# A decoder trunk on one core: the values' product moves both weight parts at once, and ScalarE scales its corrections

## What is computed

```python
qkv = h @ w_qkv
q, k, v = jnp.split(qkv, 3, axis=-1)
...
s_own = s_own - slopes[None, None, :, None] * dist_own.astype(jnp.float32)[None, :, None, :]
s_own = jnp.where((dist_own >= 0)[None, :, None, :], s_own, NEG)
...
p = jax.nn.softmax(scores, axis=-1)
...
return o @ w_o
```

## Time and profile before

| | us |
|---|---|
| median of 3 runs | 876.34 (876.16 to 876.99) |
| the profiled execution | 877.2 |
| its span, first to last instruction | 875.2 |
| PE busy | 866.4 (99%) |
| PEld busy | 756.4 (86%) |
| DVE busy | 648.8 (74%) |
| ACT busy | 467.5 (53%) |
| HBM read | 157.84 MB, 182 GB/s over the span |

### The profile page before, as it was taken

One profiled execution on the slowest core, in us unless ns is written; L12 is line 12 of the kernel. 1 busy time (PEld: TensorE's weight loads), 2 busy tenths in 40 slices (PEclk: granted clock), 3 DMA queues, 4 the chain that ended last, 5 costly groups with the idle time before them and its releaser, 6 DMA issues.

```text
span 875.2 us, 12263 instructions
## 1 busy us (share of the span) xinstructions
PE 866.4 (99%) x5103; PEld 756.4 (86%) x5103; DVE 648.8 (74%) x760; ACT 467.5 (53%) x550; POOL 22.7 (3%) x49
## 2 busy tenths in 40 slices
PE   9999999999999999999999999999999999999997
PEld 7888888888889988888888888888888988888886
DVE  6898776567987699777655697777656998777452
ACT  6765555435656665555534375555544665555441
POOL 1000005200000000000000000000000000000000
PEclk9999999999999999999999999999999999999999
DMA  7777555563644447665556566665555377565431
GB/s 238 245 243 239 192 180 169 186 206 98 220 145 145 145 143 242 193 192 181 174 187 193 180 191 197 191 191 184 172 194 172 98 240 234 185 214 184 147 118 48
DMA packets 154534, 159.67 MB, mean 182 GB/s; under 512 B 3000, under 2 KB 152816, under 8 KB 154480
## 3 DMA queue, kind: packets, MB, share of 16 engines
q1 hardware_dynamic: 154128, 158.35, 56.6%
q10 hardware_dynamic: 352, 0.55, 0.2%
HBM read 157.84 MB, written 1.05 MB: 182 GB/s over the span
## 4 chain that ended last, share of the span: by engine, by line
PE 91%; DVE 5%; DMA 1%; ACT 1%; issue 1%; SPq 0%; ACTq 0%; DVEq 0%
PE psum L455 90%; DVE w_lo L1098 2%; DMA raw<-in_ffn_w_gate_dram 1%; ACT w_hi L863 1%; DMA band<-in_x_dram 1%; PE psum L782 1%; DVE score L1393 0%; PE psum L765 0%; DVE neg_max L1398 0%; DVE neg_max L1397 0%; SPq L390 0%; PE psum L485 0%; PE psum L645 0%; DVE soft L1406 0%; DVE scratch L1374 0%
## 5 line engine op out<-in xcount | busy, mean ns | idle before, releaser
L455 PE MATMUL psum<-xg,w_hi 128*128 128x512 f32 x1536 | 484.5, 397 | 0.3 <-DVE w_lo L1098 0.3
L1098 DVE TENSOR_TENSOR w_lo<-raw,w_hi 128x2048 fp32r<-128x2048 f32 (+1 forms) x148 | 330.1, 2231 | 106.0 <-ACT w_hi L863 106.0
L455 PEld LDWEIGHTS psum<-xg,w_lo 128*128 128x128 f32 x1536 | 288.6, 188 | 68.2
L863 ACT ACTIVATE w_hi<-raw 128x2048 fp32r<-128x2048 f32 x149 | 278.0, 1867 | 116.9 <-PE psum L455 112.0
L455 PE MATMUL psum<-xg,w_lo 128*128 128x256 f32 x1536 | 301.9, 278 | 0.0
L455 PEld LDWEIGHTS psum<-xg,w_hi 128*128 128x128 f32 x1536 | 234.0, 189 | 2.7 <-issue 1.3
L455 PE MATMUL psum<-h_all,w_hi 128*128 128x512 f32 (+1 forms) x656 | 189.4, 374 | 0.0
L455 PEld LDWEIGHTS psum<-h_all,w_lo 128*128 128x128 f32 x592 | 111.4, 188 | 23.4
L455 PE MATMUL psum<-h_all,w_lo 128*128 128x256 f32 x592 | 121.8, 278 | 0.0
L455 PEld LDWEIGHTS psum<-h_all,w_hi 128*128 128x128 f32 x656 | 100.2, 189 | 0.8 <-issue 0.8
L900 ACT ACTIVATE scratch<-psum 128x512 f32<-128x512 f32 x44 | 26.1, 593 | 79.5 <-PE psum L455 79.5
(11 more groups left out here) (116 smaller groups left out, 494.0 us busy)
## 6 DMA issues: line engine op xcount, KB each, us to landing
raw<-in_ffn_w_gate_dram SPq DMA_DIRECT2D x42, 1024.0 KB, 5.3
raw<-in_ffn_w_up_dram SPq DMA_DIRECT2D x42, 1024.0 KB, 5.3
raw<-in_ffn_w_down_dram SPq DMA_DIRECT2D x24, 1024.0 KB, 5.1
raw<-in_attn_w_qkv_dram SPq DMA_DIRECT2D x12, 1024.0 KB, 5.1
raw<-in_ffn_w_down_dram SPq DMA_DIRECT2D x20, 512.0 KB, 4.2
raw<-in_ffn_w_down_dram SPq DMA_DIRECT2D x12, 768.0 KB, 4.4
raw<-in_attn_w_o_dram SPq DMA_DIRECT2D x4, 1024.0 KB, 5.7
raw<-in_ffn_w_gate_dram SPq DMA_DIRECT2D x7, 256.0 KB, 6.0
```

The source lines that it names most:

```text
L455: return nc.tensor.matmul(out, stationary, moving, start=start, stop=stop, skip_group_check=True)
L863: nc.scalar.activation(w_hi[:, n % SPL, 0:size], raw[:, n % RAW, 0:size], ACT.Copy).then_inc(hi_split, 1)
L1098: nc.vector.tensor_tensor(w_lo[:, n % SPL, 0:size], raw[:, n % RAW, 0:size], w_hi[:, n % SPL, 0:size].bitcast(f32), ALU.subtract).then_inc ...
```

## The change

`w_hi` and `w_lo` become the two halves of one tensor `w_parts`, so that a slice can take the same chunk of both. The values' product moves both parts of a chunk through the high activations in one matmul of 512 columns, and the high weights through the low activations in one of 256, which adds to the second half of the accumulator. Two chunks are taken together: two matmuls of 512, then two of 256. The accumulator is now a whole bank for each t: banks 6 and 7 (quad 0), 0 and 1 (quads 1 and 2), 4 and 5 (quad 3). ScalarE scales the second half (the corrections) into `v_sb`, `scale_v_corrections`, and VectorE scales the first half and adds the two. Waits go with the banks: V3 waits for the copies of the probabilities in banks 4 and 5 and no longer for the query scaling, and the wait for V3's scaling moves from the second scores of pass 3 to the front of `out_tile(0)`.

```diff
-        w_hi = sb("w_hi", [P, SPL, ROWS], f32r)
-        w_lo = sb("w_lo", [P, SPL, ROWS], f32r)
+        w_parts = sb("w_parts", [P, 2, SPL, ROWS], f32r)
+        w_hi, w_lo = w_parts[:, 0], w_parts[:, 1]
...
-            return psum[:, 0, t * GW:(t + 1) * GW] if j else psum[:, 6 + t, 0:GW]
+            first_bank = 6 if j == 0 else 4 if j == QUADS - 1 else 0
+            return psum[:, first_bank + t, :]
...
-                elif j:
+                elif 0 < j < QUADS - 1:
                     pe.wait_ge(qkv_scaled, 3 * j + 1)
...
-                hi, lo = col_tile(w_hi, n), col_tile(w_lo, n)
+                hi = col_tile(w_hi, n)
+                both = w_parts[:, :, n % SPL, :].rearrange("p s (k f) -> p s k f", k=DC)
                 for t in range(TT):
                     toks = slice(t * P, (t + 1) * P)
-                    for k in range(DC):
-                        out = v_acc(j, t)
-                        mm(out, xg_hi[:, k, toks], hi[:, k, :], start=(k == 0))
-                        mm(out, xg_hi[:, k, toks], lo[:, k, :])
-                        last = mm(out, xg_lo[:, k, toks], hi[:, k, :], stop=(k == DC - 1))
+                    if j == QUADS - 1:
+                        pe.wait_ge(probT_copied, QH * (j - 1) + t + 1)
+                    for k0 in range(0, DC, 2):
+                        for k in (k0, k0 + 1):
+                            mm(v_acc(j, t).rearrange("p (s f) -> p s f", s=2), xg_hi[:, k, toks], both[:, :, k, :],
+                               start=(k == 0))
+                        for k in (k0, k0 + 1):
+                            last = mm(v_acc(j, t)[:, GW:2 * GW], xg_lo[:, k, toks], hi[:, k, :], stop=(k == DC - 1))
...
             def out_tile(j, halfway=None):
                 n = ATT0 + 3 * QUADS + j
                 weights(n)
+                if j == 0:
+                    pe.wait_ge(qkv_scaled, 3 * QUADS)
...
                     pe.wait_ge(o_lo_done, j)
-                    pe.wait_ge(qkv_scaled, 3 * QUADS)
...
+            def scale_v_corrections(j):
+                act.wait_ge(consts_built, CONSTS)
+                act.wait_ge(rstd_done, 2)
+                for t in range(TT):
+                    if j == 0 and t == 0:
+                        act.wait_ge(first_v, 1)
+                    else:
+                        act.wait_ge(tile_used, ATT0 + 3 * j + 3)
+                    nc.scalar.activation(v_sb[:, j % 2, t, :], v_acc(j, t)[:, GW:2 * GW], ACT.Copy,
+                                         scale=rstd_p[:, t:t + 1]).then_inc(v_corr, 1)
...
             split_hi(ATT0 + SPL)
+            scale_v_corrections(0)
             split_hi(ATT0 + 1 + SPL)
...
+                if j < QUADS - 1:
+                    scale_v_corrections(j + 1)
                 split_hi(ATT0 + 3 * j + 4 + SPL)
                 act.wait_ge(pv_done, QH * (j + 1))
...
-                        if j == 0 and t == 0:
-                            dve.wait_ge(first_v, 1)
-                        else:
-                            dve.wait_ge(tile_used, ATT0 + 3 * j + s + 1)
-                        ins = nc.vector.tensor_scalar(v_sb[:, j % 2, t, :], v_acc(j, t),
-                                                      rstd_p[:, t:t + 1], None, ALU.mult)
+                        dve.wait_ge(v_corr, TT * j + t + 1)
+                        ins = nc.vector.scalar_tensor_tensor(out=v_sb[:, j % 2, t, :], in0=v_acc(j, t)[:, 0:GW],
+                                                             scalar=rstd_p[:, t:t + 1], in1=v_sb[:, j % 2, t, :],
+                                                             op0=ALU.mult, op1=ALU.add)
```

More of the change, by code:

```diff
@@ L226, in build_trunk @@
         first_v = sem("first_v")
+        v_corr = sem("v_corr")
         qk_corr = sem("qk_corr")
```

## The result

The changed kernel takes 890.18 us (median of 4 runs, 888.86 to 890.79) against 876.34: a ratio of 1.0154, interval 1.0142 to 1.0166. It is slower by 13.8 us, where 8.3 were forecast and 888.0 was the upper end of the range.

What follows compares the result with a forecast made beforehand. TensorE, busy 866.4 of 875.2 us, was taken as the bound. Delays of 1.72 + 2.92 + 3.66 = +8.3 us, the product's 0.74 included, took the median from 876.34 to 884.6 us; range 882.4 to 888.0.

Steps and rivals of the forecast that it cites:

- The product: Value tiles on TensorE: fewer matmuls save 0.18 us a tile, 0.74 us for four.
- Quad 0: V0's scaling comes later: a scores pause of 0.4 us less 0.18, costing nothing; uncovered 0.3 us.
- The wait chain: Passes 0 to 2: TensorE is delayed behind moves, both splits and value scaling; 1.72 + 2.92 + 3.66 = +8.3 us.
- the first rival: Clock falls from 2.4 to 1.2 GHz after pauses of 3.1 and 3.8 us; 3 us more, 887.6; chance 0.11.
- The delays added instead of overlapping: Rival of overlapping delays: pass 0's 1.72 us swallowed in pass 1, giving 882.9 us; chance 0.08.
- Not slower: Q3 and out_tile(0): split not waited for, or scaling on time anyway; no change, 875.9 us; chance 0.04.
- What was said of the profile after: Value-scaling waits 3.8, 3.1, under 0.5 us; query 2.2; PE busy slightly less; ScalarE's split 0.8 after value tile; sets 0.697.

Runs made afterwards that it cites:

- the run with filled pauses: The changed kernel with TensorE's three long pauses filled by 36 matmuls of 512 columns that nobody reads, every wait kept: 884.31 us.
- the single passes: The changed kernel with ScalarE's corrections before its last split in only pass 0, 1 or 2, behind it in the others: 879.05, 880.90 and 881.97 us.
- the run with the split in front: The changed kernel with ScalarE's last split of passes 0 to 2 put before its scaling of the corrections: 876.21 us.
- the run with VectorE's order put right: The changed kernel with VectorE scaling the values before its last split in passes 1 and 2 too, ScalarE's order kept: 882.55 us.

## Why the prediction was wrong

**The product** came as worked out, tile by tile. V3 takes 5.74 us from its start to the values step; before it started at 269.73, and the step at this row of the kernel before:

```profile
275.65 1.52 PE L782 MATMUL psum<-soft,v_sb 128*64 128x256 f32 x16
```

That is 5.92 us, 0.18 more, the figure of the prediction. The halves lying apart cost nothing that these rows show. The Trainium skill's 2.5 ns beyond a matmul's columns (TensorE: Matmul & The Clock Gate, Back-to-back issue gap), its figure for a matmul by itself, would give an estimate of 0.04 us a tile. The trace does not agree, and 0.18 holds for this stream, where every matmul has its own weight load. The forecast's sum says that 0.74 us of the product are in it, but only three tiles' 0.18 are, 0.54 us; the first tile's went into the wait for V0's scaling. The forecast of 884.6 is not touched by that.

**Quad 0** came as worked out, with a short pause in its scores, where the forecast had 0.4 us less the product's 0.18, and cost nothing: V1 starts without a wait at 226.15, against 226.24 before.

```profile
212.77 0.93 PE L459 MATMUL psum<-scratch 64*128 64x128 f32 x8 [0.23 <-DVE v_sb L1407]
```

**The wait chain** came as worked out, term by term. The first bias of pass 1 is 1.71 late (1.72 forecast), V2 1.70 (1.72); the pause before it is 2.46 (2.2), since the shorter product brings TensorE there sooner. The pause before Q3 is 3.05 (3.10), the one before output tile 0 3.66 (3.76). Without the clock's share the output tile would not be 289.32 - 277.95 = 11.37 us late but 11.37 - 3.1 = 8.3 (8.3), and the run with filled pauses gives 884.31 where 884.6 stood in the prediction.

**The step that failed is the first rival, that the clock falls in the pauses.** It had a chance of 0.11, for the reason that TensorE is dense before and between the pauses. In the trace of the change it held in all three. Its price was set at 3 us in all, between nothing and one tile; the trace has 5.4 us and the filled run 5.9, for three falls of 1.5 to 2.3 us. It was priced for the two pauses of 3.1 and 3.8 us, and the one before V2, 2.2 us by the forecast's own count, was not thought of as one. With 0.11 on it and 3 us, the range ended at 888.0 and missed. The sentence of the Trainium skill that was cited there (TensorE: Matmul & The Clock Gate, Why this matters for your kernels) spoke for the rival, and the traces agree for the pauses of 3.1 and 3.7 us. The evidence set against it was weak: the kernel before has no pause over 1.6 us, so its full clock said nothing about one of 3 us. Dense work ahead of a pause did not protect it.

**The other rivals** fell. The delays added instead of overlapping (the single passes), and the split was waited for. "Not slower" gives the time of the run with the split in front: 876.21, where the rival said 875.9.

**What was said of the profile after** was right in the waits' lengths (0.3 us short before V2), in the start of ScalarE's split behind the value tile and in the product. TensorE's busy time rose by 4.9 us instead of falling, because work at half the clock is busy for longer: that line alone shows that the waits are not the whole loss.

## What to carry to other kernels

Two small instructions added to a queue that has slack are priced by what stands behind them, not by their length: here 0.7 us of scaling carried a 1.9 us split past the end of the tile it was hidden under, and both came out on TensorE. Put what waits for the end of a product behind what does not. And on a dense TensorE count a wait of over 2 us as its own length and, behind it, 1.5 to 2.3 us of clock, as in every trace here; a few unread matmuls or transposes in the pause save that part.

## What the runs showed of the hardware

The clock and the pause before it, over the traces of all runs: after pauses of 1.1, 1.3, 1.4, 1.6, 1.7 and 2.0 us between attention tiles the clock was full; after those of 2.2, 2.5 (in three kernels), 3.1 and 3.7 us (in two each) it fell to 1.2 GHz. That is no sharp line. One execution each of the kernels with 2.2 and 2.5 us as their longest pause shows by its time and mean clock no fall, so at these lengths it goes both ways, and why stays open.

The return took longer once. Behind seven of the eight falls the clock was full again 3.1 to 4.5 us after the start of the next tile; in the change, output tile 0 had to wait 5.3 us for it. There the clock was down from some 1.5 us before that tile's start (0.80 over the pause), and that tile lost most. In the run with VectorE's order put right it was also down before V2 started, by 0.3 us, and that tile lost no more than others. Why it was down longest there stays open: no run varied it.

The Trainium skill says in its section on PE-mode transpose (TensorE: Matmul & The Clock Gate) that transposes do not engage the full clock as matmuls do. For holding a clock that is already full, the run filled with idle transposes does not agree: 884.57 us against 884.31 with matmuls and 890.18 with empty pauses. Whether transposes alone would bring a low clock back, no run here shows.
